# Moving the start addresses of the weights and the activations of a one-core transformer kernel by 16 bytes in on-chip memory

## What is computed

```python
proj = jnp.einsum('bsd,de->bse', h, w_in[l])
x = x + jnp.einsum('bse,ed->bsd', mixed, w_out[l])
return (jax.nn.silu(h @ w_gate) * (h @ w_up)) @ w_down
return (jax.nn.gelu(gate, approximate=False) * up) @ w_down
```

## Time and profile before

| | |
|---|---|
| runs | 1033.50, 1035.32, 1033.49 us |
| the profiled execution | 1033.99 us, of which the span from first to last instruction is 1032.2 us |
| TensorE busy | 1018.6 us, 99% |
| VectorE busy | 809.1 us, 78% |
| ScalarE busy | 642.1 us, 62% |
| read from DRAM | 183.96 MB, 180 GB/s over the span |
| granted TensorE clock | 1.000 of full speed |

### The profile page before, as it was taken

How to read it: one execution, slowest core, us unless ns; L and a number is a source line. 1 busy time by engine, 2 the same in 40 slices (tenths; PEclk the granted TensorE clock), 3 DMA queues, 4 the chain that set the end, 5 groups by cost and what they waited for, 6 DMA issues and landing times.

```text
span 1032.2 us, 21122 instructions
## 1 busy us (share of the span) xinstructions
PE 1018.6 (99%) x8530; PEld 990.9 (96%) x8530; DVE 809.1 (78%) x964; ACT 642.1 (62%) x864; POOL 2.7 (0%) x8
## 2 busy tenths in 40 slices
PE   9999999999999999999999999999999999999998
PEld 8888999899999999999999999998899999999998
DVE  6879976686666747998887777798998888777787
ACT  7666565466445447676785666675546668666573
POOL 0000000000000000000000000000000000000000
PEclk9999999999999999999999999999999999999999
DMA  9842464355555564644555555454433565555541
GB/s 344 276 169 83 162 217 153 123 189 191 192 181 196 205 215 154 195 157 167 205 191 182 208 203 189 174 192 164 133 117 118 181 228 189 183 209 203 185 155 68
DMA packets 30531, 186.96 MB, mean 181 GB/s; under 512 B 3735, under 2 KB 6520, under 8 KB 8840
## 3 DMA queue, kind: packets, MB, share of 16 engines
q1 hardware_dynamic: 29896, 185.05, 51.9%
q10 hardware_dynamic: 576, 1.05, 0.3%
HBM read 183.96 MB, written 1.34 MB: 180 GB/s over the span
## 4 chain that ended last, share of the span: by engine, by line
PE 78%; DVE 15%; ACT 4%; issue 2%; DMA 1%; SPq 0%; ACTq 0%; DVEq 0%
PE g L585 57%; PE d L585 20%; DVE w_lo L1579 5%; ACT hy_scores L1079 1%; ACT w_hi L1079 1%; DVE x L1576 1%; DMA raw<-weights 1%; DVE sq_sum L1576 1%; DVE newton L1573 1%; DVE newton L1583 1%; PE d L588 0%; DVE gla_w L1573 0%; DVE p_both L1583 0%; DVE gla_o L1573 0%; ACT rough L1079 0%
## 5 line engine op out<-in xcount | busy, mean ns | idle before, releaser
L1579 DVE TENSOR_TENSOR w_lo<-raw,w_hi 128x2048 fp32r<-128x2048 f32 (+1 forms) x175 | 389.2, 2227 | 89.9 <-ACT w_hi L1079 89.1
L1079 ACT ACTIVATE w_hi<-raw 128x2048 fp32r<-128x2048 f32 (+1 forms) x174 | 326.3, 1877 | 144.7 <-PE g L585 87.8
L585 PE MATMUL g<-f_both,w_hi 128*128 128x256 f32 x1408 | 241.2, 275 | 3.2 <-DVE conv_in L1573 3.2
L585 PEld LDWEIGHTS g<-f_both,w_hi 128*128 128x128 f32 x1408 | 212.0, 188 | 3.6 <-issue 3.5
L585 PE MATMUL g<-f_both,w_lo 128*128 128x256 f32 x704 | 193.7, 275 | 0.0
L585 PE MATMUL d<-hid_hi,w_hi 128*128 (+1 forms) x528 | 145.2, 275 | 0.0
L585 PE MATMUL d<-hid_lo,w_hi 128*128 (+1 forms) x528 | 145.2, 275 | 0.0
L585 PE MATMUL d<-hid_hi,w_lo 128*128 (+1 forms) x528 | 145.2, 275 | 0.0
L585 PEld LDWEIGHTS g<-f_both,w_lo 128*128 128x128 f32 x704 | 132.2, 188 | 0.0
L585 PE MATMUL g<-x_both,w_hi 128*128 128x256 f32 x704 | 120.0, 275 | 0.0
L585 PEld LDWEIGHTS g<-x_both,w_hi 128*128 128x128 f32 x704 | 106.0, 188 | 0.1
(11 more groups left out here) (365 smaller groups left out, 1971.1 us busy)
## 6 DMA issues: line engine op xcount, KB each, us to landing
raw<-weights SPq DMA_DIRECT2D x168, 1024.0 KB, 4.8
bias_tab<-bias_dram SPq DMA_DIRECT2D x8, 192.0 KB, 7.5
x<-x_t ACTq DMA_DIRECT2D x4, 256.0 KB, 5.5
raw<-weights SPq DMA_DIRECT2D x4, 256.0 KB, 6.8
raw<-weights SPq DMA_DIRECT2D x2, 512.0 KB, 7.5
mem_t<-mem_t SPq DMA_DIRECT2D x1, 1024.0 KB, 8.9
out<-x SPq DMA_DIRECT2D x3, 256.0 KB, 2.2
hy_swap<-hy_qk SPq DMA_DIRECT2D x4, 128.0 KB, 6.0
```

Source lines behind the costliest of these rows:

```text
L585: return pe.matmul(out, lhsT, rhs, start=start, stop=stop, skip_group_check=True)
L1079: return act.activation(out, in_, func, **kw)
L1579: return dve.tensor_tensor(out, a, b, ALU.subtract)
```

## The change

Stationary weights begin 4 columns (16 bytes) into their slot. Every activation tensor that was at 112 bytes is at 128, and `MOVED` follows. The token-major weights, which began at column 28, begin at column 32, at 128 bytes. In bytes modulo 256 from `W_AT`:

| | stationary | moving |
|---|---|---|
| 158 chunks, before | weights 0 | activations 112 |
| 158 chunks, after | weights 16 | activations 128 |
| 12 token-major chunks, before | activations 112 | weights 112 |
| 12 token-major chunks, after | activations 128 | weights 128 |

`probs_m`, `mem_k`, `q_mem` and `mem_v` stay where they are. No instruction is added, removed or moved in the order.

```diff
 DISTANCE = 112
-FURTHER_COLS = DISTANCE // 4
+FIRST_COL = 4
+FURTHER_COLS = FIRST_COL + DISTANCE // 4
 W_SLOT = CHUNK + P
...
 def start_col(c):
 
-    return FURTHER_COLS if isinstance(c, int) and c in FURTHER else 0
+    return FURTHER_COLS if isinstance(c, int) and c in FURTHER else FIRST_COL
...
-        IN = parts_at("in_both", A_AT + DISTANCE)
-        MEM = parts_at("mem_both", B_AT + DISTANCE)
+        IN = parts_at("in_both", A_AT + DISTANCE + 4 * FIRST_COL)
+        MEM = parts_at("mem_both", B_AT + DISTANCE + 4 * FIRST_COL)
...
-        MOVED = (DISTANCE - (H - W_AT)) % 256
+        MOVED = (DISTANCE + 4 * FIRST_COL - (H - W_AT)) % 256
```

More of the change, by code:

```diff
@@ L210, in parts_at @@
             return both[:, :, 0, :], both[:, :, 1, :]
-        IN = parts_at("in_both", A_AT + DISTANCE)
-        MEM = parts_at("mem_both", B_AT + DISTANCE)
[L214 to L224, removed]
+        IN = parts_at("in_both", A_AT + DISTANCE + 4 * FIRST_COL)
+        MEM = parts_at("mem_both", B_AT + DISTANCE + 4 * FIRST_COL)
+        OUT = parts_at("out_both", A_AT + DISTANCE + 4 * FIRST_COL)
+        CO = parts_at("co_both", A_AT + DISTANCE + 4 * FIRST_COL)
+        X0 = parts_at("x0_both", B_AT + DISTANCE + 4 * FIRST_COL)
+        HY = parts_at("hy_both", A_AT + DISTANCE + 4 * FIRST_COL)
+        HO = parts_at("ho_both", B_AT + DISTANCE + 4 * FIRST_COL)
+        F1 = parts_at("f1_both", A_AT + DISTANCE + 4 * FIRST_COL)
+        P1 = parts_at("p1_both", B_AT + DISTANCE + 4 * FIRST_COL)
+        GLA = parts_at("gla_both", A_AT + DISTANCE + 4 * FIRST_COL)
+        GO = parts_at("go_both", B_AT + DISTANCE + 4 * FIRST_COL)
+        F2 = parts_at("f2_both", A_AT + DISTANCE + 4 * FIRST_COL)
+        P2 = parts_at("p2_both", B_AT + DISTANCE + 4 * FIRST_COL)
         sq = sb("sq", [2, 2 * T])
```

## The result

The changed kernel takes 1070.1 us (median of four runs, 1065.5 to 1072.2) against 1033.6 us: a ratio of 1.0336, with a 95% interval of 1.0318 to 1.0354. It is slower by 36.5 us. The profiled execution took 1072.2 us, with a span of 1070.4.

A forecast was written before the change was run, and what follows sets the result against it. The prediction took TensorE, by its step from matmul to matmul, to bound the kernel. With all terms at 0 the forecast stayed at the median of 1033.5 us, range 1005 to 1046 us.

The forecast's parts named there:

- What bounds the kernel: Whole kernel: TensorE, busy 1018.6 of 1032.2 us, so only the step between matmul starts and the stops change the time much.
- the writers' term of 0: ScalarE's and VectorE's writes of `w_hi` and `w_lo`: starting 16 past a multiple of 32 lengthens no write; 0 us.
- The step of the 7584 matmuls: Matmuls of the 158 chunks: time between starts stays 113.3 ns; term 0, bounds -48 and +36 us.
- the shift by 192: Cross-attention's scores: both operands lie 192 bytes further, same difference of 112, still 113.3 ns, so place in steps of 64 does nothing.
- the 16-column case: Matmuls with 16 stationary columns: load 94 ns instead of 188, step still 113.3 ns, so 272 cycles belong to the moving stream.
- Rival 3: Chunk matmuls: stream never falls into step, 5.0 ns on 7234 matmuls, 1070 us, chance 0.18; mild form 1036 to 1046, 0.08.
- Rival 1: Moving stream: slow because of its odd start, so aligning it gives 1014 us, or 985 at 107 ns; chance 0.22.
- Rival 2: Matmuls behind breaks and token-major ones: falling out of step never happens, saving 1.8 and 1.5 us; 1030.2 us, chance 0.12.
- The step of the 288: Token-major matmuls, at about 232 ns: difference of places stays 0, so no change; term 0, bounds -1.5 and +1.5 us.

The follow-up runs named there:

- scan_shift: Kernel before with both operands of six phases moved by 4, 8, 16, 48, 64 or 96 bytes, difference kept at 112; 1039.8 us in one run.
- w0_a128: Changed kernel with the stationary weights of the 158 chunks back at 0, activations still at 128; 1066.7 us, ratio 1.0306.
- w64_a128: Changed kernel with the stationary weights of the 158 chunks at 64 in place of 16, activations at 128; 1046.0 us, ratio 1.0134.
- the two scans: Stationary weights of 28 chunks each at a place of its own, on the kernel before (1040.1 us) and the changed kernel (1070.1 us), one run each.
- tok_w128: Kernel before with only the token-major weights, the moving operand there, moved from 112 to 128; 1033.2 us, ratio 0.9991.

## Why the prediction was wrong

- **What bounds the kernel** was right. All of the loss is in the step of the matmuls; the writers' term of 0 held, and the stops gave 4 us back.
- **The step of the 7584 matmuls** is the term that failed. I put it at 0, between bounds of -48 and +36 us, because the shift by 192 was free and the 16-column case was in step, and called these the nearest rows. It measured +44.9 us in gaps, the 5.9 ns a matmul a little over the upper bound of 5.0: the streams behind a break are at 118.3 ns, and this pair settles at 120.0 in most of the kernel. The error in the choice was to read "a shift by 192 is free" as "a shift is free". 192 is a multiple of 32, and 16 is not; in scan_shift 64 and 96 were free, 16 and 48 were not. Nothing in the trace of before had a pair shifted by another amount, so the row did not bear on the question that it was used for. Nor did the 16-column row. In the changed kernel that stream, whose loads still take 94 ns, has a mean step of 116.6 ns over 22 gaps; in w0_a128, with both its operands at the same places, 113.6. A shorter load does not keep the stream in step, so the row did not tie the 272 cycles to the moving operand alone.
- **Rival 3**, at 0.18, is what happened, and its price was nearly right: 1070 us forecast, 1070.1 measured. That it agrees to 0.1 us is luck: the step cost 44.9 us and not 36, the shorter stops and the token-major gain took back 5.4, and the four executions lie between 1065.5 and 1072.2. Its sign to look for, triples 0.35 to 0.36 us apart all through, is what the timeline shows. Its mechanism was only half right. It blamed the odd stationary operand; w0_a128 has it at 0 and is as slow, and w64_a128 is at 113.3 or at 117.8 with the same operands.
- **Rival 1** (an odd moving start makes the stream slow) is refuted: with an aligned moving operand the stream got slower (118.8 ns in w0_a128), and (64, 128) and (192, 128), also aligned, are at 113.3 ns at best. The 262 cycles of the Trainium skill ("TensorE: Matmul & The Clock Gate", Back-to-back issue gap), which it gives for 256 columns as the gap of a matmul by itself, were reached at none of the 56 pairs of the two scans; this float32r stream has 272 at best.
- **Rival 2** (never out of step, 1030.2 us) did not come: the lowest median of all runs is 1033.2 us (tok_w128), not measurably below the kernel before. The skill's sentence that TensorE never waits for its port ("SBUF — State Buffer", SBUF: two separate sides) gave "no change" and is not borne out as a rule on speed: with the same instructions, addresses alone moved the step by up to 11 ns.
- **The step of the 288** was inside its bounds of 1.5 us: -1.1 us. I had the wrong cause in rival 3's support; their excess went away with the moving operand's place alone.
- **The range** left out just the case that came, on the ground of a chance of 0.18 in full. With a row for either step, in step and out of step, and no row for the new pair, that chance was too low: of the 56 pairs scanned, 50 were never seen at 113.3 ns in their chunk.

## What to carry to other kernels

A stream of float32r matmuls with a load for each had a step that hangs on where both operands begin, and a good pair was an exception: of 56 read in one chunk each, five stayed at 113.3 ns and a sixth was there up to a break. When a tuned pair is in place, move both operands by a multiple of 32 bytes or not at all, and before a shift is called free, ask whether the row that says so was shifted by the same remainder. Measure a candidate pair in all phases, behind every kind of break and in more than one execution, not in one chunk: two pairs that looked perfect in one chunk were 1.2 and 1.3% slower in the kernel.

## What the runs showed of the hardware that was not expected

- Matmuls of one form, at full clock and with nothing to wait for, keep one rhythm for over 100 us, whatever the other engines and the transfers do. Its mean can be 272, 280, 283 to 285 or 288 cycles for the same 256 columns (113.3, 116.7, 117.8 to 118.7, 120.0 ns); single gaps in it repeat a pattern, in w0_a128 from 115 to 123 ns.
- A pair of places can have two such rhythms or more: 113.3 and 117.8 ns at (64, 128), 118.7 and 120.0 at (0, 128) in w0_a128, 118.7, 116.7 and 113.3 at (0, 144). A break of two small matmuls switched from one to the other in two of five places. A change of the moving tensor can do it without a break, as at (0, 160). At (0, 112) every stretch came to 113.3 ns. The changed kernel went through 120.0, 118.3 and 116.7 ns, each time behind a break, which also fits its runs being spread from 1065 to 1072 us; that the spread comes from this was not shown.
- Moving both operands by 4 or 8 bytes was the worst, 122.2 and 124.5 ns, in one run.

What stays open is what meets what. The step does not depend on whether VectorE, ScalarE and the DMA engines are busy, which leaves TensorE's own accesses, above all the loads and the moving stream. That these two disturb each other is inferred from the two places counting together; a stream without loads was not tried. Nor was a third or fourth break of another length, which would tell what a break has to do to choose the good rhythm.
